# An attention layer on one core: a new order in the first two token tiles and at the seam between attention and output projection

## The reference

```python
xn = rms_norm(x, norm_in)
proj = xn @ w_in        # 2464 columns: a_q a_k a_v a_g b_cq b_ckv b_kr b_g
q, k = rope(rms_norm(a_q)), rope(rms_norm(a_k))       # 8 query heads, 2 kv heads, width 64
y_a = softmax(q k^T / 8) a_v
qb = rms_norm(rms_norm(b_cq) @ w_uq)                  # 4 heads, width 96, last 32 rotated
kv = rms_norm(b_ckv) @ w_ukv                          # k_nope and v of the 4 heads
y_b = softmax(qb kb^T / sqrt(96)) vb
h = x + concat(y_a * silu(a_g), y_b * silu(b_g)) @ w_out
```

## Time and profile before

| | us |
|---|---|
| median of 3 runs | 1621.65 (1619.77 to 1623.49) |
| the profiled execution | 1625.9 |
| its span, first to last instruction | 1624.1 |
| PE busy | 1530.8 (94%) |
| DVE busy | 1171.4 (72%) |
| ACT busy | 1050.2 (65%) |
| POOL busy | 581.4 (36%) |
| PE, mean granted clock | 0.979 of full speed |

### The profile page before, as it was taken

How to read it: one execution, slowest core, us unless ns; L and a number is a source line. 1 busy time by engine, 2 the same in 40 slices (tenths; PEclk the granted TensorE clock), 3 DMA queues, 4 the chain that set the end, 5 groups by cost and what they waited for, 6 DMA issues and landing times. The chain is left out here.

```text
span 1624.1 us, 36745 instructions
## 1 busy us (share of the span) xinstructions
PE 1530.8 (94%) x13138; PEld 880.7 (54%) x13138; DVE 1171.4 (72%) x1620; ACT 1050.2 (65%) x1374; POOL 581.4 (36%) x504
## 2 busy tenths in 40 slices
PE   6899999999991899999999999999999999978999
PEld 3455555555550465665566566656655665643444
DVE  6655464645554989988998898899889989862332
ACT  7644454444431788888888888888888888841110
POOL 0100000000000566665666666566656666710000
PEclk9999999999995999999999999999999999999999
DMA  8476655675448323233243323223322433279894
GB/s 298 140 161 124 166 142 130 141 166 123 118 109 202 128 63 76 69 81 64 64 95 81 64 61 85 62 74 80 81 64 61 98 74 67 71 173 221 243 234 119
DMA packets 354846, 189.70 MB, mean 117 GB/s; under 512 B 174480, under 2 KB 335760, under 8 KB 354800
## 3 DMA queue, kind: packets, MB, share of 16 engines
q1 hardware_dynamic: 329232, 173.31, 43.6%
q10 hardware_dynamic: 24672, 14.88, 3.9%
q0 software_dynamic: 896, 0.93, 0.5%
HBM read 119.16 MB, written 40.93 MB: 99 GB/s over the span
## 5 line engine op out<-in xcount | busy, mean ns | idle before, releaser
L1179 POOL TENSOR_TENSOR p_pl<-p_p,p_ph 128x512 f16<-128x512 f32 x384 | 503.2, 1317 | 405.1 <-ACT p_ph L1215 346.5
L1236 DVE TENSOR_REDUCE p_part<-p_mx 128x2 f32<-128x1024 f32 x384 | 468.2, 1219 | 86.6 <-PE p_mx L1333 68.4
L1206 ACT ACTIVATE p_p<-p_st 128x1024 f32<-128x1024 f32 x384 | 391.3, 1019 | 115.7 <-PE p_st L1365 58.2
L869 PE MATMUL p_ring<-p_w_hi,p_xT 128*128 128x512 f16 (+3 forms) x1536 | 388.7, 341 | 15.5 <-DVE p_xT L699 12.2
L1215 ACT ACTIVATE p_ph<-p_p 128x1024 f16<-128x1024 f32 x336 | 355.3, 1057 | 18.3
L1264 DVE TENSOR_TENSOR p_pl<-p_p,p_ph 128x512 f16<-128x512 f32 x384 | 327.0, 852 | 3.1 <-ACT p_ph L1215 2.4
L869 PE MATMUL p_ring<-p_w_lo,p_xT 128*128 128x512 f16 (+3 forms) x768 | 261.8, 341 | 0.0
L869 PEld LDWEIGHTS p_ring<-p_w_hi,p_xT 128*128 128x128 f16 x1536 | 152.0, 99 | 135.1 <-DVE p_xT L699 8.8
L1397 PE MATMUL p_acc<-p_vas,p_ph 128*128 128x129 f16 x2048 | 207.9, 221 | 0.0
L1398 PE MATMUL p_acc<-p_vas,p_pl 128*128 128x65 f16 x2048 | 201.0, 193 | 0.0
L1397 PEld LDWEIGHTS p_acc<-p_vas,p_ph 128*128 128x128 f16 x2048 | 180.6, 97 | 36.4 <-issue 14.3
(11 more groups left out here) (129 smaller groups left out, 2038.7 us busy)
## 6 DMA issues: line engine op xcount, KB each, us to landing
p_vbs<-scratch_vb SPq DMA_DIRECT2D x16, 1028.0 KB, 6.4
p_xin<-in_x SPq DMA_DIRECT2D x16, 512.0 KB, 5.9
p_xcol<-in_x_cols SPq DMA_DIRECT2D x16, 512.0 KB, 5.6
scratch_g<-p_g SPq DMA_DIRECT2D x16, 512.0 KB, 4.4
p_kb<-scratch_kb SPq DMA_DIRECT2D x32, 256.0 KB, 5.3
p_xr<-in_x SPq DMA_DIRECT2D x16, 512.0 KB, 4.5
out<-p_res SPq DMA_DIRECT2D x16, 512.0 KB, 3.1
out_gt<-scratch_g ACTq DMA_DIRECT2D x14, 512.0 KB, 5.0
```

Source lines behind the costliest of these rows:

```text
L869: last = pe.matmul(ring_t[:, 0:w], a, b, start=(k == 0 and m == 0), stop=(k == len(steps) - 1 and m == len(terms) - 1))
L1179: pool.tensor_tensor(pl[:, s % NP, 1, :], p32[:, s % N32, QB:], ph[:, s % NP, 1, :], ALU.subtract).then_inc(s_lop, 1)
L1206: act.activation(p32[:, s % N32, :], st[:, s % 2, :, :].rearrange("p a b -> p (a b)"), ACT.Exp, scale=scale).then_inc(s_exp, 1)
L1236: dve.tensor_reduce(part[:, e // MPAIRS % 3, 2 * c:2 * c + 2], mx[:, :, :], AX, ALU.max).then_inc(s_red, 1)
```

## The change

**First two tiles.** In ScalarE's and VectorE's `first_pair`, the high and low halves of tile 0's `x` now come ahead of the first split of weights; the low split of piece 1 is divided around `x_scale(1)`, and `x_lo(1)` comes ahead of the split of piece 2; `x_stat(2)` comes behind the split of piece 5, and several copies out of PSUM change places with halves of the splits of pieces 6 and 7. In SyncE's list the columns of tile 1 are loaded behind piece 1 (this load waits for `x_lo(0)`), and the first transposes of latents behind the loads that used to follow them; the stores of gates and values and the load of the columns of tile 3 change places. On GpSimd `spread_rstd` of tile 2 now stands ahead of the waits for all weights. TensorE's list is as it was.

**Seam.** In the last turn of the attention loop VectorE gates output tile 0 after step 17's `lo`, and makes its low half in step 20; ScalarE writes its high half in step 18. Behind the loop VectorE gates output tile 1, ahead of the last `denominator`, and ScalarE writes tile 1's high half behind the last `copy_acc`. In stage 3, VectorE makes tile 1's low half between the two halves of the split of `w_out`.

**Order of terms.** In each half of an output tile, the 16 matmuls with the high half of `y` now come first and the 8 with its low half after them, and TensorE waits for the turned low half only ahead of those 8 in the first half of the tile.

```diff
@@ SyncE, first_pair
                 load_w(1)
+                load_cols(1)
                 ...
                 load_w(3)
-                load_cols(1)
                 load_w(4)
                 load_w(5)
-                turn_latents(0)
                 load_x(2)
                 load_cols(2)
-                load_w(6)
                 load_trig(0)
                 load_trig(1)
                 sp.dma_start(gains[:, :], g_heads.partition_broadcast(P)).then_inc(s_gains, 16)
+                turn_latents(0)
+                load_w(6)
+                load_w(7)
                 load_x(3)
-                load_w(7)
                 turn_latents(1)
                 store_v(0)
                 load_x(4)
+                store_g(0)
                 store_v(1)
-                store_g(0)
+                load_cols(3)
                 turn_z(0)
-                load_cols(3)
                 store_g(1)
@@ GpSimd
+            spread_rstd(pool, 2)
             pool.wait_ge(s_whi, rows_before[-1])
             pool.wait_ge(s_wlo, rows_before[-1])
...
-            for t in range(2, TILES):
+            for t in range(3, TILES):
                 spread_rstd(pool, t)
@@ ScalarE, first_pair
                 x_stat(0, 0)
+                x_hi(0, 0)
                 act.wait_ge(s_gin, 16)
-                split_hi(0, 0)
-                x_hi(0, 0)
-                split_hi(0, 1)
+                split_all(0)
                 x_stat(1, 1)
                 split_all(1)
+                x_hi(1, 1)
                 cq_out(0, 0)
                 act.wait_ge(s_const, 32)
                 split_all(2)
-                x_hi(1, 1)
                 ckv_out(0, 0)
...
-                x_stat(2, 0)
                 split_all(5)
                 aq_out(0, 0)
+                latent_hi(1, 1)
+                x_stat(2, 0)
+                aq_out(1, 1)
+                akv_out(0, 0)
                 split_hi(6, 0)
-                aq_out(1, 1)
-                latent_hi(1, 1)
+                up_out(0, 0)
                 split_hi(6, 1)
-                akv_out(0, 0)
-                split_hi(7, 0)
-                up_out(0, 0)
                 heads_sq(0, 0)
                 v_hi(0)
+                akv_out(1, 1)
+                split_hi(7, 0)
+                gate(0, "ag")
                 split_hi(7, 1)
                 heads_dev(0)
-                akv_out(1, 1)
-                gate(0, "ag")
                 x_stat(3, 1)
                 up_out(1, 1)
@@ VectorE, first_pair
                 x_scale(0, 0)
+                x_lo(0, 0)
                 dve.wait_ge(s_gin, 16)
-                split_lo(0, 0)
-                x_lo(0, 0)
-                split_lo(0, 1)
+                split_all(0)
                 x_rstd(1, 1)
-                split_all(1)
+                split_lo(1, 0)
                 x_scale(1, 1)
+                split_lo(1, 1)
+                x_lo(1, 1)
                 dve.wait_ge(s_const, 32)
                 split_all(2)
-                x_lo(1, 1)
                 ...
+                split_all(5)
+                latent_lo(1, 1)
                 x_rstd(2, 0)
-                split_all(5)
-                split_lo(6, 0)
-                latent_lo(1, 1)
-                split_lo(6, 1)
-                split_lo(7, 0)
+                split_all(6)
                 heads_sum(0)
                 v_lo(0)
-                split_lo(7, 1)
+                split_all(7)
                 heads_chain(0, 0)
...
                 v_lo(1)
+                x_lo(2, 0)
                 z_lo(0, 0)
-                x_lo(2, 0)
@@ stage 2, ScalarE
                 for s in range(HALF):
                     step(i, s, first)
+                    if last and s == 18:
+                        high(0)
+            def high(t):
+                act.wait_ge(o.s_yg, t * 2 + 2)
+                act.activation(o.yh[:, t, :], o.yg[:, t, :], ACT.Copy).then_inc(o.s_yh, 1)
...
-            act.wait_ge(o.s_yg, 2)
-            act.activation(o.yh[:, 0, :], o.yg[:, 0, :], ACT.Copy).then_inc(o.s_yh, 1)
             copy_acc(N - 1, 2, False)
+            high(1)
@@ stage 2, VectorE
-                    if last and s in SPLIT_AT:
-                        split_w(SPLIT_AT.index(s))
+                    if last and s == 17:
+                        gate(0)
+                    if last and s == 19:
+                        split_w(0)
+                    if last and s == 20:
+                        dve.wait_ge(o.s_yh, 1)
+                        dve.tensor_tensor(o.yl[:, 0, :], o.yg[:, 0, :], o.yh[:, 0, :], ALU.subtract).then_inc(o.s_yl, 1)
+                    if last and s == 21:
+                        split_w(1)
...
             split_w(2)
-            dve.wait_ge(o.s_y[0], 48)
...
-            dve.tensor_tensor(o.yl[:, 0, :], o.yg[:, 0, :], o.yh[:, 0, :], ALU.subtract).then_inc(o.s_yl, 1)
+            gate(1)
+            denominator(N - 1, 2, False)
             split_w(3)
-            denominator(N - 1, 2, False)
@@ stage 3, VectorE, tile
                 if first and h == 0:
-                    gate(1, 1, 0, True)
-                    split_lo(1)
+                    split_lo(1, range(0, 2))
+                    return
+                if first:
+                    dve.wait_ge(s_yh, 2)
+                    dve.tensor_tensor(yl[:, 1, :], yg[:, 1, :], yh[:, 1, :], ALU.subtract).then_inc(s_yl, 1)
+                    split_lo(1, range(2, 4))
+                    gate(2, 0, 1)
+                    residual(0, 0, 0, True)
                     return
@@ stage 3, TensorE, tile
                 pe.wait_ge(s_yt[h], i * 16 + 16)
-                pe.wait_ge(s_ytl[h], i * 16 + 16)
...
-                        for m, (s, w) in enumerate(((0, w_hi), (0, w_lo), (1, w_hi))):
-                            mm = pe.matmul(po[h][c][:, :], yT[:, h, s, k, :], w[c][:, k, :],
-                                           start=(k == 0 and m == 0), stop=(k == KT - 1 and m == 2))
+                        pe.matmul(po[h][c][:, :], yT[:, h, 0, k, :], w_hi[c][:, k, :], start=k == 0, stop=False)
+                        pe.matmul(po[h][c][:, :], yT[:, h, 0, k, :], w_lo[c][:, k, :], start=False, stop=False)
+                    if c == 0:
+                        pe.wait_ge(s_ytl[h], i * 16 + 16)
+                    for k in range(KT):
+                        mm = pe.matmul(po[h][c][:, :], yT[:, h, 1, k, :], w_hi[c][:, k, :], start=False, stop=k == KT - 1)
```

More of the change, by code:

```diff
@@ L1441, in phase3 @@
         po = [[ps(f"po{b}{c}", [P, 512]) for c in range(2)] for b in range(2)]
[L1443 removed]
+        s_wlo, s_y, s_g, s_sg, s_yg = o.s_wlo, o.s_y, o.s_g, o.s_sg, o.s_yg
         s_yh, s_yl, s_yt, s_ytl = o.s_yh, o.s_yl, o.s_yt, o.s_ytl
         s_x = [sem("x_loaded0"), sem("x_loaded1")]
+        s_whi1 = sem("w_hi_second_half")
         s_po = sem("out_in_psum")
@@ L1508, in tile @@
                     act.wait_ge(o.s_yst, SEQ // QB * HB * 48)
-                    load_g(act, o, 2, 0, G)
-                    load_y(act, o, 2, 0, YA, YB)
-                    return
-                act.wait_ge(s_yg, t * 2 + 2)
                 if not first:
+                    act.wait_ge(s_yg, t * 2 + 2)
                     act.wait_ge(s_yt[h], i * 16)
-                act.activation(yh[:, h, :], yg[:, h, :], ACT.Copy).then_inc(s_yh, 1)
-                if not (last and h == 1):
+                    act.activation(yh[:, h, :], yg[:, h, :], ACT.Copy).then_inc(s_yh, 1)
+                if not (first and h == 0) and not (last and h == 1):
                     silu(t + 1, 1 - h, i if h == 0 else i + 1)
@@ L1525, in _, with gate @@
         def _(dve):
-            def gate(t, h, i, early):
+            def gate(t, h, i):
                 dve.wait_ge(s_y[h], i * 48 + 48)
                 dve.wait_ge(s_sg, t + 1)
-                if not early:
-                    dve.wait_ge(s_yh, t - 1)
-                    dve.wait_ge(s_yl, t - 1)
+                dve.wait_ge(s_yh, t - 1)
+                dve.wait_ge(s_yl, t - 1)
                 dve.tensor_tensor(yg[:, h, 0:512], ya[:, h].rearrange("p h d -> p (h d)"), gt[:, h, 0:512], ALU.mult).then_inc(s_yg, 1)
@@ L1545, in residual, with split_lo @@
                                              op0=ALU.mult, op1=ALU.add).then_inc(s_res, 1)
-            def split_lo(c):
-                for k in range(KT // 2):
+            def split_lo(c, part):
+                for k in part:
                     ks, cols = slice(2 * k, 2 * k + 2), slice(c * 512, (c + 1) * 512)
-                    dve.wait_ge(s_whi, c * (KT // 2) + k + 1)
+                    dve.wait_ge(s_whi1, k + 1)
                     dve.scalar_tensor_tensor(out=w_lo[c][:, ks, :], in0=w_raw[:, ks, cols], scalar=WS,
@@ L1555, in tile @@
                 if first and h == 0:
-                    gate(1, 1, 0, True)
-                    split_lo(1)
+                    split_lo(1, range(0, 2))
[6 more added lines that the diff above has]
+                    residual(0, 0, 0, True)
                     return
```

(8 more changed lines are left out.)

13 lines of the change are left out of this document (6 added, 7 removed).

## The result

| | us | ratio to before, 95% interval |
|---|---|---|
| before, median of 5 runs beside it | 1622.08 (1619.77 to 1624.17) | |
| changed kernel, median of 5 runs | 1607.98 (1607.67 to 1612.51) | 0.9921 [0.9903, 0.9938] |
| forecast | 1600.0 (1594.5 to 1608) | |

The change is faster, by 12.8 us by the ratio and 14.1 by the medians; 21.7 were forecast. The profiled execution of the changed kernel took 1607.9 us, its span is 1606.1. Against the profiled execution of before (1625.9) that is 18.0 us less, and the two traces show where they lie. The seam is counted from the start of VectorE's `lo` of step 17 in the last turn, behind which the change puts the gate, to the first matmul of stage 3.

The account below looks back on a forecast made before the run. TensorE, busy for 94% of the span, was taken as the bound, so only its idle or half-speed time counts. Front 12.5 plus seam and stage 3 9.2 gave 21.7 us: 1621.65 - 21.7 = 1600.0 us, range 1594.5 to 1608.

Parts of the forecast that it names:

- 12.5 forecast: First two tiles: 11.3 us from an earlier tile 2 plus 2.5 for the clock, less 1.3 for small stops.
- The limit by ScalarE's list: First two tiles: ScalarE's work order sets the pace; uq(1) copied out at 58.8, tile 2 starting at 74.4 instead of 85.67.
- a new one of about 2.4 us appears ahead of `bg(0)`: First two tiles: TensorE's waits of 1.78 and 3.30 us for copies vanish and one stop of about 2.4 us replaces them.
- 5.0 us at half speed cost 2.5: Tile 2 in stage 1: TensorE's 1.2 GHz stretch after the 4.01 us stop cost 2.5 us, counted as gain.
- The first rival: First two tiles: front gives 7 us because ScalarE or VectorE waits for later-loaded weights; 1605.5 us, chance 0.17.
- at 0.68 each it costs nothing: Seam: tile 0's gate, two operations of 0.68 us, fits into VectorE's idle 2.22 us for free.
- The prediction's alternative of 3.2 us for the gate: Seam: if GpSimd and VectorE share SBUF interfaces, the gate takes 3.2 us instead of 1.4; seam gives 0 to 1.
- Its 2.8 us for `yl(0)`: Seam: upper price of tile 0's low half beside GpSimd's work, 2.8 us at most, where 1.5 was taken.
- Tile 2's transposes are issued behind the residual and the store of tile 0; they move by 2.3 us with it, to 1450.3: Start of stage 3: tile 2's high transpose lands at 1463.4, a stop of 4.3 us; tile 2 starts 5.2 us earlier.
- 4.0 and shared the other 3.0 of the stage with the seam part: Stage 3: 4.0 us from later tiles' stops ending, 3.0 from the stage's start to tile 2.
- So these stops end: Later tiles of stage 3: TensorE's idle 2.7 us in 100 disappears, as the low transpose may land 3.5 us later.
- The rival that the DMA queues limit the later tiles: Stage 3: landings stretch, the pace stays 10.7 and the 4.0 us are lost; 1604.0 us, chance 0.13.

Follow-up runs that it names:

- e1: The kernel before, unchanged, run once more with a profile of its own; 1624.1 us, ratio to before 1.0002.
- e3: The kernel before with only the seam part (moved gate, high and low halves of output tiles 0 and 1); 1627.6 us, ratio to before 1.0027.
- e4: The kernel before with only the new order of terms and the later wait for the low half; 1614.5 us, ratio to before 0.9947.
- e9: The changed kernel, but SyncE turns tile 1's latents between the two halves of piece 7, ahead of load_x(3); 1613.0 us, ratio to before 0.9953.
- e13: The changed kernel, but ScalarE copies akv(1) out behind the first half of the split of piece 7; 1609.1 us, ratio to before 0.9919.
- e8: The changed kernel, but VectorE makes yl(0) behind the loop's last lo instead of in step 20; 1608.4 us, ratio to before 0.9918.
- e6: The changed kernel, but SyncE turns tile 1 only after two loads of gates, the second tile 2's, have landed; 1610.4 us, ratio to before 0.9919.
- e7: The changed kernel, but SyncE issues the loads of tile 2's gates and attention results in stage 2; 1603.3 us, ratio to before 0.9881.
- e10: The changed kernel, but GpSimd's spread_rstd(2) is put back behind the waits for all weights and the memsets; 1614.4 us, ratio to before 0.9969.
- e2: The kernel before with only the new order in the first two tiles; 1611.8 us, ratio to before 0.9940.

## Why the prediction was off

The sign was right, and so was where the front and the order of terms gain; the gain at the seam did not come, and 12.8 us stand where 21.7 were forecast. Three steps failed: a wait that the sum left out, in the front; a price, at the seam; and the landing of loads, at the start of stage 3. Part of the miss is chance in the trace that the sum was made on.

**The front: 12.5 forecast, 9.7 by the run alone, 9.3 between the means of the traces.** The limit by ScalarE's list held to 1.4 us. The step "a new one of about 2.4 us appears ahead of `bg(0)`" failed. The stop is 3.4 to 5.4 us, and in the changed kernel it stands ahead of `uq(1)`, where TensorE waits for the turned latents. The sum had put the landing of these transposes at nothing; it took 9.1 us in the median, against 3.1 before. Also, "5.0 us at half speed cost 2.5" was read from one execution. In e1, the same kernel as before, TensorE waited 3.47 us for `x_lo(2)` and went on at full clock:

```profile
85.28 0.33 PE L869 MATMUL p_ring<-p_w_hi,p_xT 128*128 128x384 f16 x1 [3.47 <-DVE p_xT L699]
```

It started the attention 2.7 us earlier. In e3 and e4, with the same front, the clock fell for 3.2 and 3.3 us, so the loss was 2.5, 0, 1.6 and 1.7 us in four executions. In the changed kernel it is the new stop that is followed by half the clock, so what was booked as a gain is paid again. The Trainium skill, "TensorE: Matmul & The Clock Gate", Part 1, says that the point at which the gate moves varies from run to run. The traces agree. The first rival (the front gives half, because ScalarE waits for weights) did not happen: in the changed kernel's trace ScalarE waits for no weights in the first 60 us. But the DMA queue that it named seems to be what limits the stretch (e9, e13).

**The seam: the step "at 0.68 each it costs nothing" failed.** The gate of tile 0 was priced at 0.68 an operation, as it runs with GpSimd idle, and put into 2.22 us of idle time; it took 3.2 in all, and `yl(0)` 2.18 where 1.5 were taken. The attention's matmuls so ended 2.6 us later behind the `lo` of step 17 than before, not 1.5 later. And from there to stage 3 it is 3.88 us, not 3.2: the last split was priced with GpSimd idle too (1.94 against 1.23). The prediction's alternative of 3.2 us for the gate was right, and e8 bears out the reason, since the same `yl(0)` takes 1.21 us with GpSimd idle. (Its 2.8 us for `yl(0)` does not follow from the rows it names: 1.58 against 2.85 for three gives 1.23 x 1.66 = 2.0 us, near the 2.18.) The Trainium skill, "GPSIMD Engine Reference", section 1, says that GpSimd's SBUF interfaces are shared with VectorE, and that the two contend where VectorE reads two SBUF inputs. These rows agree. The seam gained 0.6 us in this trace and in e6, and lost about 1 in the five others with the same seam (e3, e7, e9, e10, e13).

**Stage 3: the sum was near, its split was wrong.** "Tile 2's transposes are issued behind the residual and the store of tile 0; they move by 2.3 us with it, to 1450.3" failed: they were issued 16.5 us into the stage, not 14.1. The step left out that the transposes of tile 1, moved to the front of the stage, meet the loads of tile 2. The order of terms alone takes stage 3 from 183.2 (mean of before, e1 and e2) to 174.4, 9 us where the prediction gave it 4.0 and shared the other 3.0 of the stage with the seam part. The three traces behind that mean run from 179.9 to 185.5, as tile 2's stop is 0.38, 3.11 or 5.12 us in them, so the 9 is rough. The seam part took some 5 of these back. That was the missing rival: the seam part costs, and the rest gains more without it. "So these stops end" held: 100.00 us of 100. The rival that the DMA queues limit the later tiles is out: the pace rose at a share of 0.83, where it had been 0.85.

**The base.** The profiled execution of before was 4 us slower than its median, that of the changed kernel was not. I took a sum made on the slow one off the median, so its chance losses were booked as gains: the 8.0 us between forecast and median are 3.7 between the traces and 4.3 here.

## What to carry to other kernels

A transfer that becomes possible earlier also becomes a rival of the loads issued beside it: when a step moves ahead, look at what its DMAs push back, and what stands in order behind the instruction that waits for those. An operation moved into an engine's idle time must be priced from a row with the same neighbours at work. And a stop or half-clock stretch read from one execution should be looked up in a second one before it is booked as a gain.

## What the runs showed of the hardware

- A product of two 128x512 tiles in float32 took VectorE 0.68 us with GpSimd idle and 1.64 beside its work; a subtraction of two 128x1024 tiles 1.21 and 2.18. The split's high half, which reads one 128x1024 tile (`TENSOR_SCALAR`), took 0.66 and 1.65 in the changed kernel (at 1423.91 and 1414.37), so an operation with one tensor input can be slowed too.
- Plain loads of 512 and 256 KB took 5.9 and 6.1 us to land, and 9.6 and 10.1 when one DMA transpose was issued 0.1 us ahead of the first and another 1.5 us behind the last. With the transposes held back they took 5.9 and 6.1 again.
- TensorE's clock after the same stop of 2.73 us stayed at 2.4 GHz in two executions and fell to 1.2 in five, at a cost of 1.6 us each. After 3.88 us ahead of stage 3 the first matmul still ran at full clock in six of seven (0.38 us, against 0.58 in before); in these six the fall came 0.3 to 1.1 us later.
- The changed front started the attention anywhere from 499.0 to 503.8 in seven executions of the same code. In the three late ones, from 502.2 on, the DMA share from 60 to 95 us is 0.93 to 0.94 at 100 to 102 GB/s, in the four early ones, up to 500.4, 0.55 to 0.59 at 113 to 121; in the late ones TensorE also waits 0.3 to 2.1 us for a later tile's latents near 128. The share alone doesn't decide it: e13, which differs by one copy, has 0.95 and starts at 500.9. Why a front falls into one or the other isn't settled.
